# Forget terms over all rows, residual tiles between evictions, a pause moved, in a two-block transformer kernel

## What is computed

```python
x = x + mixed @ w_out[l]
return rmsnorm(x, final_g)                      # first block: the residual of the second

proj = h @ w_in                                 # q_a k_a v_a q_b k_b v_b f_logit g_a g_b
cum_f = jnp.cumsum(log_f.astype(jnp.float32), axis=-1)
logits = jnp.einsum('bhqd,bhkd->bhqk', qb, kb) * scale
logits = logits + cum_f[:, :, t0:t1, None] - cum_f[:, :, None, :t1]
causal = jnp.arange(t1)[None, :] <= jnp.arange(t0, t1)[:, None]
probs = jax.nn.softmax(jnp.where(causal, logits, NEG_INF), axis=-1)
```

## Time and profile before

| | us |
|---|---|
| median of 3 runs | 2908.21 |
| lowest, highest | 2905.38, 2914.47 |
| the profiled execution | 2921.34 |
| its span, first to last instruction | 2919.5 |
| TensorE matmuls busy | 2854.0 (98%) |
| GpSimd busy | 2286.3 (78%) |
| ScalarE busy | 1297.9 (44%) |
| VectorE busy | 1071.2 (37%) |
| granted TensorE clock, mean | 0.986 |

### The profile page before, as it was taken

How to read it: one execution, slowest core, us unless ns; L and a number is a source line. 1 busy time by engine, 2 the same in 40 slices (tenths; PEclk the granted TensorE clock), 3 DMA queues, 4 the chain that set the end, 5 groups by cost and what they waited for, 6 DMA issues and landing times.

```text
span 2919.5 us, 58628 instructions
## 1 busy us (share of the span) xinstructions
PE 2854.0 (98%) x24150; PEld 2815.1 (96%) x24150; DVE 1071.2 (37%) x1572; ACT 1297.9 (44%) x1523; POOL 2286.3 (78%) x925
## 2 busy tenths in 40 slices
PE   7999989999999999999999999999999999999998
PEld 7999989899899899999999999999999999999998
DVE  6123365353321301224599993120302112034322
ACT  6354542654433344344444664343444434344333
POOL 6787730589667678888799548898998989889996
PEclk9999989999999899999999999999999999999999
DMA  6555420355445345555445556556565655656653
GB/s 247 172 174 186 156 71 15 103 186 187 145 158 172 119 158 189 186 199 189 159 173 187 208 225 227 184 207 218 187 229 182 229 184 197 230 188 215 230 193 124
DMA packets 85843, 524.60 MB, mean 180 GB/s; under 512 B 8672, under 2 KB 23136, under 8 KB 24544
## 3 DMA queue, kind: packets, MB, share of 16 engines
q1 hardware_dynamic: 68400, 489.38, 47.9%
q10 hardware_dynamic: 17328, 33.56, 3.1%
HBM read 504.03 MB, written 18.87 MB: 179 GB/s over the span
## 4 chain that ended last, share of the span: by engine, by line
PE 54%; POOL 25%; issue 19%; DVE 1%; ACT 1%; POOLq 0%; DVEq 0%
PE banks L1434 54%; POOL wlo L413 25%; POOLq L412 0%; DVE T L851 0%; PE banks L1553 0%; POOLq L417 0%; DVE dec L1058 0%; ACT L519 0%; ACT L518 0%; DVE at__97 L1066 0%; DVE qt L1078 0%; DVE dec L1077 0%; DVE at__97 L1076 0%; ACT expr L625 0%; DVE dec L1080 0%
## 5 line engine op out<-in xcount | busy, mean ns | idle before, releaser
L413 POOL TENSOR_TENSOR wlo<-raw,whi 128x1024 fp32r<-128x1024 f32 x920 | 2281.6, 2499 | 562.5 <-ACT whi L447 554.3
L447 ACT ACTIVATE whi<-raw 128x1024 fp32r<-128x1024 f32 x916 | 946.8, 1057 | 825.9 <-PE banks L1434 818.2
L1434 PE MATMUL banks<-xhi,whi 128*128 128x256 f32 x4672 | 640.6, 280 | 11.2 <-DVE va L1165 6.9
L1434 PE MATMUL banks<-xhi,wlo 128*128 128x256 f32 x4672 | 636.0, 279 | 7.1 <-POOL wlo L413 7.1
L1434 PE MATMUL banks<-xlo,whi 128*128 128x256 f32 x4672 | 635.9, 279 | 0.0
L1434 PEld LDWEIGHTS banks<-xhi,whi 128*128 128x128 f32 x4672 | 584.2, 189 | 13.6 <-DVE va L1165 7.1
L1434 PEld LDWEIGHTS banks<-xhi,wlo 128*128 128x128 f32 x4672 | 582.8, 189 | 8.6 <-POOL wlo L413 8.6
L1434 PEld LDWEIGHTS banks<-xlo,whi 128*128 128x128 f32 x4672 | 583.3, 189 | 0.0
L1434 PE MATMUL banks<-hid_lower,whi 128*128 128x256 f32 x2048 | 274.1, 276 | 0.1
L929 DVE TENSOR_TENSOR X<-banks,X 128x256 f32 (+1 forms) x112 | 47.4, 423 | 573.7 <-PE banks L1434 573.7
L1434 PEld LDWEIGHTS banks<-hid_lower,whi 128*128 128x128 f32 x2048 | 251.2, 188 | 0.4 <-PE banks L1434 0.3
(11 more groups left out here) (362 smaller groups left out, 2356.2 us busy)
## 6 DMA issues: line engine op xcount, KB each, us to landing
raw<-in_w_exp SPq DMA_DIRECT2D x256, 1024.0 KB, 4.8
raw<-in_w_in SPq DMA_DIRECT2D x132, 1024.0 KB, 4.9
raw<-in_w_out SPq DMA_DIRECT2D x32, 1024.0 KB, 4.9
raw<-in_w_br SPq DMA_DIRECT2D x16, 1024.0 KB, 4.9
raw<-in_w_q SPq DMA_DIRECT2D x16, 1024.0 KB, 4.9
gates<-gst ACTq DMA_DIRECT2D x16, 1024.0 KB, 4.9
gch<-gates ACTq DMA_DIRECT2D x7, 2048.0 KB, 12.8
raw<-in_w_kv SPq DMA_DIRECT2D x8, 1024.0 KB, 9.6
```

Of the source, the lines that this page charges most:

```text
L413: pool.tensor_tensor(wlo[:, s, :, :], raw[:, j, h * HALF:(h + 1) * HALF, :], whi[:, s, :, :].bitcast(F32), ALU.subtract).then_inc(lo_ready, 1)
L447: act.activation(whi[:, (2 * j + h) % 4, :, :], raw[:, j, h * HALF:(h + 1) * HALF, :], ACT.Copy).then_inc(hi_ready, 1)
L1434: return nc.tensor.matmul(o, lhsT, rhs, start=start, stop=stop, **k)
```

## The change

`fq` and `fkh` get all 128 rows; `fq` is cleared whole before its rows are written, and the existing clearing of `fkh` covers 128 rows by its new shape, so rows 40 to 127 are zero in both. The block that scales the 16 tiles of X is cut up: tile k is scaled behind the eviction of unit 16 + k of IN2. The wait for the last of them moves behind the evictions of unit 63. The pause leaves the segment that starts IN2 (unit 77 of all) and the segment of IN2 that begins at its unit 68 gets one (unit 145 of all).

```diff
-        fq = at("fq", [40, S], sm + 128 + K)
+        fq = at("fq", [P, S], sm + 128 + K)
         fk = at("fk", [40, S], sm + 128 + 2 * K)
-        fkh = at("fkh", [40, 8, S], o_T + 8 * K)
+        fkh = at("fkh", [P, 8, S], o_T + 8 * K)
...
-            scale_tiles(range(KT), X, lambda k: gain_col(G_FINAL, k), rstd1, X, sg("x2_done"))
-            dve.wait_ge(sg("x2_done"), 4)
+            def x2_tile(k):
+                scale_tiles((k,), X, lambda k: gain_col(G_FINAL, k), rstd1, X, sg("x2_done"))
...
                     ins.then_inc(evac[u % 2], 1)
+                    if n0 + k < 2 * KT:
+                        x2_tile(n0 + k - KT)
                     if k in after:
                         after[k]()
...
                 step(dve.tensor_scalar(fk[:], psf[0:40, 1024:1024 + S], -1.0, None, ALU.mult))
-                step(dve.tensor_copy(fq[:], psf[0:40, 1024:1024 + S]))
+                step(dve.memset(fq[:], 0.0))
+                step(dve.tensor_copy(fq[0:40], psf[0:40, 1024:1024 + S]))
                 dve.memset(fq[32:40], 1.0).then_inc(sg("cumf"), 1)
...
             evict(48, 16, sga, None, {0: forget_sums, 4: fx_maxima, 7: lambda: fx_shares(0), 9: lambda: fx_shares(1)})
+            dve.wait_ge(sg("x2_done"), 4)
             keep_values(fx_vtk, sg("fx_vt_mm"), sg("fx_vt"))
...
-            segment(U_IN2, 16, False, bhi, blo, tiles(0), lambda: tile_sums(6, by_tile(0), True), paused=1)
+            segment(U_IN2, 16, False, bhi, blo, tiles(0), lambda: tile_sums(6, by_tile(0), True))
...
-            segment(U_IN2 + 68, 12)
+            segment(U_IN2 + 68, 12, paused=1)
```

## The result

The changed kernel took 2882.26 us in the median of 4 runs (2877.89 to 2897.14), against 2911.34 for the kernel before, now in 4 runs: ratio 0.9911, 95% interval 0.9884 to 0.9938, that is 26 us less. A second series (`e5_whole_again`) gave 0.9915 (0.9896 to 0.9934). Forecast were 2884.4 us and 23.8 us less. The total is right. The experiments show that its terms are not all right: rows and tiles together measured 17.8 us instead of 23.8, and the pause, which I put at nothing, about 7.

The account below looks back on a forecast made before the run. TensorE was taken as the bound; tiles 9.8, rows 14.0 and pauses 0 summed to 23.8 us less, from a median of 2908.2 to 2884.4 us, range 2871 to 2896.

Parts of the forecast that it names:

- (1): Second projection, unit 18: tiles scaled singly remove TensorE's 6.9 us idle and the half clock behind it, gaining 9.8 us.
- the slack: Softplus steps before the suffix sums: 4.8 us to spare against 0.8 to 5.0 added by two tiles, cost taken 0.
- (2): Forgetting-attention logits: fq and fkh over 128 rows take 10.30 us instead of 22.62, and 1.7 less behind them; gain 14.0 us.
- the upper bound of 2.1: Unit 51's wait for unit 49's eviction: 0 taken, 2.1 us at most if fkh's product misses GpSimd's gap.
- (3): Pause moved from unit 77 to unit 145: 0.33 us goes and comes, pace unchanged, net 0.
- rival A: Pause at unit 145 sets the fast pace to the end of OUT2, 9.5 us less: 2875; chance 0.22.
- losing was excluded: From unit 145 to the end of OUT2 a pause cannot worsen the pace, since it is already the slow one.
- B: Clock still falls in the new logits, costing 1.3 us there and 7.2 behind: 2893 us; chance 0.10.
- C: Logits: the 0.2 us comes from a second matmul adding to the first's sum; rows gain nothing: 2898 us; chance 0.06.
- D: The experts' stage, fast before, starts in the slow pace, +45 us: 2930 us; chance 0.04.
- E: VectorE's queue behind units 24 and 25 stalls TensorE at most 0.3 us, plus 2.1 at unit 51; no chance given.

Follow-up runs that it names:

- e5_whole_again: The changed kernel, unaltered, measured again against the kernel before: 2887.15 us (7 runs), ratio 0.9915.
- e2: The kernel before with only the tiles of X spread over the evictions of units 16 to 31: 2900.89 us (10 runs), ratio 0.998.
- e10: e7 with pauses at units 77, 145, 149 and 157: 2885.63 us (4 runs), ratio to the kernel before 0.9895.
- e6: The kernel before with only the pause moved from unit 77 to unit 145: 2903.05 us (12 runs), ratio 0.9974.
- e7: The changed kernel with X tiles in twos behind units 16 to 23 and fkh cleared behind unit 42: 2879.60 us, ratio to the kernel before 0.9897.
- e8: The changed kernel with a wait at unit 148 for evictions up to unit 147 replacing unit 145's pause: 2893.48 us, ratio to the kernel before 0.9946.
- e9: The changed kernel without the pause at unit 145: 2895.95 us (6 runs), ratio to the kernel before 0.9939.
- e3: The kernel before, 40 rows kept, logits matmuls grouped so the row count changes 4 times instead of 32: 2898.52 us (1 run).
- e4: The changed kernel with 30 pauses put between the logits matmuls, 128 rows kept: 2896.29 us (1 run).

## Why the prediction was right, and where it was not

**(1) Tiles, 9.8 us: right, but for a wait that I put at nothing.** The hole went as worked out, and with it the half clock behind it: in the trace of before the clock reads 0.50 from 738 to 744 us, 0.61 from 744 to 745 and 1.00 from 745 to 750. From the second half of unit 0 of IN2 to the scores the traces read, at the slow pace and with the pause of unit 77, 120.52 us with the hole (before) and 110.63 without (`e2`, `e10`): 9.9 less. At the fast pace and without that pause they read 116.43 (`e6`) and 106.29 (`e7`, `e8`, `e9`): 10.1 less. The suffix sums give back 0.9, which I had at 0 to 0.3. The step that failed there is the slack: I counted two tiles, 0.8 to 5.0 us, against 4.8, but the products behind the tiles start in GpSimd's subtracts anew (0.69 us became 2.30, 1.40 became 2.42), and the chain came 5.6 us late. 9.0 us remain, and 5.8 (2 to 10) was measured.

**(2) Rows, 14.0 us: the mechanism right, the size too large.** The gap of 0.2 us at each change, 6.3 us in all, is shown (`e3`, `e2`). The half clock on top, which I took as given by one trace, is missing in one of five traces (`e2`) and shorter in another (`e6`). The mean of the five is 20.8 us, 10.5 above 10.29. From the logits to unit 60 the change saves 0.6 us on the mean instead of 1.7: in two of the four traces with half clock there, a fast pace behind it makes up the loss. And unit 51 costs 1.7, within the upper bound of 2.1 that I gave, though I took 0; it was the copy into `fkh` (1.22 us before, 3.13 after), not the product behind it (4.40 and 4.39), that met GpSimd. That makes 9.4, and 7.0 (4 to 10) was measured. What brings the clock down, changes of row count and few rows together or something else, stays open: either alone held 1.00 in one trace each.

**(3) The pauses, 0: wrong.** The step that failed is "I take 0, as the one at unit 77". One trace of a pause that left the pace alone was taken for its nature. It is rival A, given 0.22, that holds in a part of the executions, three of six traces: about 7 us in two comparisons (`e5` against `e9`, and `e6`), of the 8.5 that one turned trace gains. That is more than half of 8.5, but the intervals allow it. That losing was excluded holds for this place, but not for pauses: `e2` and `e10` lose the fast pace at one.

**The rivals.** B (clock low in the new logits) is not seen in any of the eight traces with 128 rows, `e4`'s gaps included. C is refuted by the changed kernel's own logits, which still add to the same sums without a gap. D (slow experts) is not seen in any trace; the changed kernel's 2000 to 2060 hold 532 matmuls as before. E came true in both places: 0.9 us, over its bound of 0.3, and 1.7, under its bound of 2.1.

So the forecast of the total is right partly by luck, on two errors that cancel: 23.8 for rows and tiles, 17.8 (14 to 22) measured and 18.4 by the traces; 0 for the pause, about 7 measured. Where TensorE is the bound and its pace can change at stops, one trace of a kernel is one sample: the kernel before took 120.52 us for the stretch before the scores in one trace and 116.4 in two others, by pace alone.

## What to carry to other kernels

Take the size of a clock or pace loss from several profiles of the same kernel, and only the mechanism from one; and compare traces that are at the same pace. Keep the row count of successive matmuls constant, by grouping them or by padding with zeros (a change between 40 and 128 rows cost 0.2 us here), and keep whatever an idle VectorE can do out of chains that a PSUM eviction is queued behind (0.9 and 1.7 us here). A forecast of a sum is tested by its parts: run the change without each of them before calling the reasons right.

## What the runs showed of the hardware

- A change between 40 and 128 rows costs TensorE 0.20 us (`e2`) to 0.21 us (`e3`) at full clock; the matmuls themselves take the same over either, 2.81 and 2.82 us for sixteen of 128 columns (`e3`).
- In these traces TensorE streams the units' 256-column matmuls at one of two paces at full clock, 113.3 or 117.8 ns by their starts, for hundreds of matmuls on end. In the traces of before, after and `e7` each change of pace lies at a gap of 0.2 us or more between two starts, or at other matmuls than the units'. A wait for its own last matmul, 0.33 us, can switch it either way (three of six at unit 145, three of seven at unit 77); a stop with 0.5 us of idle, where it waits for an eviction (`e8`), and six with 6.9 to 7.7 us (the hole) did not. What sets the outcome was not found.
- How long a VectorE step takes beside GpSimd's 2.4 us subtracts depends on when it starts: the same 128x256 product took 0.47, 0.70 and 2.30 us in the changed kernel, the 8x2048 copy 1.22 (before), 2.60 (`e7`) and 3.13 (after).
- A memset on VectorE took the same over few rows and over 128: 0.27 us for 8x256 (before) and 128x256 (after), 1.76 for 40x2048 (before) and 128x2048 (after).
